# An encoder layer with a mixture of experts on one core: products that nobody reads on TensorE while it waits for the router, with four other edits around the router, the first tile and the last expert

## What is computed

```python
h = h + merged @ w_o
h = h + hier_moe(rms_norm(h, norm_ffn), w_router_group, ..., w_gate, w_up, w_down)

# hier_moe: cg, fe are the logits of 4 groups and of 8 experts in each
g_idx = jnp.argmax(cg, axis=-1)
p_e = jax.nn.softmax(fe[rows, g_idx], axis=-1)
top_p, top_i = lax.top_k(p_e, 2)
# for each of the 32 experts e, on the rows that chose it
y_e = (silu(x @ w_gate[e]) * (x @ w_up[e])) @ w_down[e]
```

## Time and profile before

| | us |
|---|---|
| median of 3 runs | 943.34 (941.81 to 944.59) |
| the profiled execution | 944.84 |
| its span, first to last instruction | 942.6 |
| PE busy | 828.6 (88%) |
| DVE busy | 269.3 (29%) |
| ACT busy | 196.9 (21%) |
| POOL busy | 133.6 (14%) |
| bytes moved by DMA | 251.41 MB, mean 267 GB/s |

### The profile page before, as it was taken

One profiled execution on the slowest core, in us unless ns is written; L12 is line 12 of the kernel. 1 busy time (PEld: TensorE's weight loads), 2 busy tenths in 40 slices (PEclk: granted clock), 3 DMA queues, 4 the chain that ended last, 5 costly groups with the idle time before them and its releaser, 6 DMA issues. The chain is left out here.

```text
span 942.6 us, 10773 instructions
## 1 busy us (share of the span) xinstructions
PE 828.6 (88%) x4578; PEld 519.3 (55%) x4578; DVE 269.3 (29%) x497; ACT 196.9 (21%) x336; POOL 133.6 (14%) x154
## 2 busy tenths in 40 slices
PE   4999998999999999997899987787877888687976
PEld 3777895679999999785434432222222333222322
DVE  4555138854313434355111110101010411001010
ACT  4423237846121313111000000000000000000000
POOL 5010061000000001210222211211111111112101
PEclk9999999989999999998699998989889989989998
DMA  9142216000203043964999999999999999999993
GB/s 321 28 141 90 90 58 226 2 2 1 105 31 134 1 179 139 404 251 154 368 413 410 410 410 410 415 406 415 413 411 410 417 415 413 409 411 416 407 416 119
DMA packets 51616, 251.41 MB, mean 267 GB/s; under 512 B 7433, under 2 KB 7481, under 8 KB 26992
## 3 DMA queue, kind: packets, MB, share of 16 engines
q1 hardware_dynamic: 39344, 228.92, 59.8%
q0 software_dynamic: 11184, 21.79, 7.9%
q10 hardware_dynamic: 1040, 0.00, 0.1%
HBM read 242.30 MB, written 15.59 MB: 274 GB/s over the span
## 5 line engine op out<-in xcount | busy, mean ns | idle before, releaser
L1377 PE MATMUL ps<-ring,xT 128*64 128x512 f32 x768 | 188.9, 648 | 50.7 <-DMA ring<-in_w_up_dram 49.7
L1377 PEld LDWEIGHTS ps<-ring,xT 128*64 128x64 f32 x768 | 60.4, 149 | 176.0 <-issue 112.0
L1767 DVE COPY hidT<-ps 128x256 f32<-128x256 f32 x32 | 13.6, 425 | 401.8 <-PE ps L1386 401.8
L1395 PE MATMUL ps<-high_ring,hidT 128*64 128x512 f32 x512 | 118.6, 604 | 7.2 <-DMA high_ring<-in_w_down_dram 2.4
L1070 PE MATMUL ps<-hnT_hi,ring_r 128*128 128x288 f32 x512 | 91.6, 296 | 0.1
L1377 PE MATMUL ps<-high_ring,xT 128*64 128x512 f32 x256 | 65.0, 667 | 18.8 <-DMA high_ring<-in_w_up_dram 18.8
L1070 PEld LDWEIGHTS ps<-hnT_hi,ring_r 128*128 128x128 f32 x512 | 75.9, 188 | 0.5 <-issue 0.5
L987 ACT ACTIVATE silu<-ps,rstd 128x256 f32<-128x256 f32 x32 | 15.2, 474 | 292.1 <-PE ps L1377 292.1
L1395 PEld LDWEIGHTS ps<-high_ring,hidT 128*64 128x64 f32 x512 | 40.6, 138 | 63.2 <-issue 60.7
L717 POOL DMA_INDIRECT out_y_dram<-yb,idx x32 | 50.3, 1572 | 147.0 <-ACT yb L991 143.2
L711 POOL DMA_INDIRECT xg<-hn_dram,idx x32 | 33.5, 1048 | 259.7 <-PE ps L1367 238.1
(11 more groups left out here) (281 smaller groups left out, 1032.3 us busy)
## 6 DMA issues: line engine op xcount, KB each, us to landing
high_ring<-in_w_down_dram SPq DMA_DIRECT2D x32, 2048.0 KB, 35.0
ring<-in_w_gate_dram SPq DMA_DIRECT2D x24, 2048.0 KB, 34.2
ring<-in_w_up_dram SPq DMA_DIRECT2D x24, 2048.0 KB, 35.2
high_ring<-in_w_gate_dram SPq DMA_DIRECT2D x8, 2048.0 KB
high_ring<-in_w_up_dram SPq DMA_DIRECT2D x8, 2048.0 KB
ring<-in_w_in_dram SPq DMA_DIRECT2D x7, 2048.0 KB, 8.7
ring<-in_w_o_dram SPq DMA_DIRECT2D x2, 2048.0 KB, 10.5
ring<-in_w_in_dram SPq DMA_DIRECT2D x2, 1024.0 KB, 8.1
```

The costliest lines, as they stand in the source:

```text
L1377: last = pe.matmul(out, xT[:, odd, k % (KD // 2), k // (KD // 2), :], w[:, k, :, s * F // 2:(s + 1) * F // 2], start=(k == 0), stop=(k == ...
L1395: last = pe.matmul(banks(6 + odd, 0, BANK, SLOTS, s * SLOTS), hidT[:, k % (KF // 2), k // (KF // 2), :], w[:, k, s * HALF_D:(s + 1) * HALF ...
```

## The change

Five edits.

1. **Products that nobody reads.** `keep_awake(n)` issues n products of two bfloat16 constants into a bank of PSUM that nothing reads: 62 in all, between the router's last steps.
2. **First tile in halves.** Tile 0 is scaled, rounded and subtracted in two halves of four chunks, ahead of the weights' pieces; chunks 0 to 3 wait for the first half only. The transposes of the next tile move inside a tile's products (after chunk 2, in tile 0 after chunk 4).
3. **First rows selected.** Expert 0's rows no longer come from the gather: `slots_first` makes a one-hot matrix `sel` per tile on VectorE, `select_tile` multiplies it with h in SBUF, ScalarE copies the rows (`xg_first`), and `wide(1)` uses them. `load_wide(4)` then stands ahead of `load_down(2)`.
4. **Last mixer tiles by halves.** The second-half products of tiles 3 and 4 are interleaved, so that chunks 0 to 3 of all tiles are done early. These chunks free the first half of pair 3's place and down 0's place (the merged arrays are now laid out in two halves), and SyncE loads both after `half_used`. The router's steps are spread anew; the product of choice and row number moves from VectorE to GpSimd (`mark_tokens`), and two instructions of `route` become one.
5. **Last expert.** `load_wide(31)` moves ahead of `load_down(29)`, and the products of gate and up of the last expert ahead of down of the expert two before it, with its own buffer `hidT_last`.

The core of the diff:

```diff
@@ SyncE
             load_wide(2)
+            sp.wait_ge(half_used, 1)
+            load_down(0)
+            wide_half(3, 0, first_half_loaded)
             sp.wait_ge(o_made, 2 * TILES)
-            load_down(0)
-            load_wide(3)
+            wide_half(3, 1, pair_loaded[3])
             load_down(1)
+            sp.wait_ge(wide_made, 1)
+            load_wide(PAIR_RING)
             sp.wait_ge(weights_made, 1)
             load_down(2)
-
-            sp.wait_ge(wide_made, 1)
-            load_wide(PAIR_RING)
...
+                    if e == EXPERTS - 2 * DOWN_RING:
+                        sp.wait_ge(wide_made, EXPERTS - PAIR_RING)
+                        load_wide(EXPERTS - 1)
@@ GpSimd
+            pool.wait_ge(eT_made, 1)
             pool.memset(xg[:, :, :], 0.0).then_inc(xg_init, 1)
...
-            gather(0)
             gather(1)
@@ ScalarE
+            act.wait_ge(rows_selected, 1)
+            act.activation(xg_first[:, :], ps[:, SELECT_BANK, :], ACT.Copy).then_inc(first_out, 1)
@@ TensorE
+            mixer_rows(3, 1, range(1))
+            turn_h(3, 0)
+            mixer_rows(3, 1, range(1, 2))
+            turn_h(2, 1)
+            mixer_rows(3, 1, range(2, 4))
+            route_tile(2, 1, 7)
+            mixer_rows(4, 1, range(0, 2))
+            route_tile(3, 0, 6)
+            rank_tile(1)
+            turn_h(4, 0)
+            mixer_rows(4, 1, range(2, 4)).then_inc(half_used, 1)
+            table_tile(0)
+            mixer_rows(3, 1, range(4, 6))
+            rank_tile(2)
+            mixer_rows(3, 1, range(6, KD))
+            route_tile(4, 0, 8)
+            mixer_rows(4, 1, range(4, 6))
+            turn_h(3, 1)
+            mixer_rows(4, 1, range(6, KD))
+            route_tile(3, 1, 9)
...
+            def select_tile(t):
+                n = TOK_ROWS[t]
+                pe.wait_ge(sel_ready, t + 1)
+                for s in range(2):
+                    last = pe.matmul(banks(SELECT_BANK, 0, BANK, SLOTS, s * SLOTS), sel[0:n, (t - 1) % TILES, :],
+                                     h[0:n, t, s * HALF_D:(s + 1) * HALF_D], start=(t == 0), stop=(t == TILES - 1),
+                                     skip_group_check=True)
...
+            def keep_awake(n):
+                for _ in range(n):
+                    pe.matmul(banks(4, 0, P), ident_b[:, :], ones[:, :], start=True, stop=True)
+
+            select_tile(0)
+            table_tile(1)
+            turn_h(4, 1)
+            select_tile(1)
+            route_tile(4, 1, 10)
+            select_tile(2)
             table_tile(2)
-            rank_tile(TILES - 1)
-            table_tile(TILES - 2)
-            table_tile(TILES - 1)
+            keep_awake(14)
+            rank_tile(3)
+            keep_awake(14)
+            select_tile(3)
+            keep_awake(14)
+            rank_tile(4)
+            select_tile(4)
+            keep_awake(8)
+            table_tile(3)
+            table_tile(4)
+            pe.wait_ge(first_out, 1)
+            for c in range(KD // 2):
+                last = pe.transpose(banks(3, c * P, (c + 1) * P), xg_first[:, c:HALF_D:KD // 2], ident[:, :])
+            last.then_inc(eT_made, 1)
+            keep_awake(12)
+            pe.wait_ge(pair_loaded[0], 32)
+            wide(1, 0, 0, xT_first[:, :, :, :])
...
+                if e == EXPERTS - 3:
+                    turn_hidden(e + 2, 1 - odd)
+                    pair_there(e + 2)
+                    wide(e + 3, odd, (e + 2) % PAIR_RING)
@@ VectorE
+            take_hn_first(0)
             split_low("k", (0,))
-            dve.wait_ge(gain_loaded, 16)
-            take_hn(0)
-            low_hn(0)
+            low_hn_first(0)
+            take_hn_first(1)
+            low_hn_first(1)
             split_low("k", (1,))
...
+            take_turned(4, 0, 8)
+            add_mixer(3, 1)
+            take_turned(3, 1, 9)
+            add_mixer(4, 1)
+            slots_first(2)
+            slots(2, 1)
+            take_turned(4, 1, 10)
+            route(3)
+            route(4)
+            for t in (3, 4):
+                slots_first(t)
+                slots(t, 1)
```

More of the change, by code:

```diff
@@ L729, in scatter @@
                 scatter_rows(idx[:, e:e + 1], e % 2, scattered[e % 2])
-            gather(0)
             gather(1)
-            for e in range(2):
-                reached(eT_made, e + 1)
-                gather(e + 2)
+            gather(2)
+            reached(eT_made, 2)
+            gather(3)
             for e in range(EXPERTS):
@@ L1303, in rank_tile @@
                 pe.wait_ge(hot_ready, t + 1)
-                if t >= 1 and t < TILES - 1:
-                    pe.wait_ge(slots_ready, min(t, TILES - 2))
-                out = banks(6, t * EXPERTS, (t + 1) * EXPERTS)
+                before = [s for s in range(t) if RANK_BANK[s] == RANK_BANK[t]]
+                if before:
+                    pe.wait_ge(slots_ready, before[-1] + 1)
+                out = banks(RANK_BANK[t], t * EXPERTS, (t + 1) * EXPERTS)
                 for s in range(t):
@@ L1324, in _ @@
                 mixer_rows(t, 0, range(KD))
-            for t in range(TILES):
+            for t in range(TILES - 2):
                 mixer_rows(t, 1, range(1))
@@ new lines, in _, with wide @@
+            turn_h(3, 1)
+            mixer_rows(4, 1, range(6, KD))
+            route_tile(3, 1, 9)
+            def wide(done, odd, pair, x=None):
+                pe.wait_ge(eT_out, done)
+                x = xT[:, odd, :, :, :] if x is None else x
+                w = pairs[pair].rearrange("p m (k n) -> p k m n", n=F)
+                for k in range(KD):
+                    for s in range(2):
+                        out = banks(2 + odd, 0, BANK, SLOTS, s * SLOTS).rearrange("p (m n) -> p m n", m=2)
+                        last = pe.matmul(out, x[:, k % (KD // 2), k // (KD // 2), :],
+                                         w[:, k, :, s * F // 2:(s + 1) * F // 2], start=(k == 0), stop=(k == KD - 1),
+                                         skip_group_check=True)
+                last.then_inc(wide_made, 1)
@@ L1368, in turn_x @@
                 last.then_inc(eT_made, 1)
-            def wide(done, odd, pair, chunks=range(KD)):
-                pe.wait_ge(eT_out, done)
-                w = pairs[pair].rearrange("p m (k n) -> p k m n", n=F)
-                for k in chunks:
-                    for s in range(2):
-                        out = banks(2 + odd, 0, BANK, SLOTS, s * SLOTS).rearrange("p (m n) -> p m n", m=2)
-                        last = pe.matmul(out, xT[:, odd, k % (KD // 2), k // (KD // 2), :],
-                                         w[:, k, :, s * F // 2:(s + 1) * F // 2], start=(k == 0), stop=(k == KD - 1),
-                                         skip_group_check=True)
-                if chunks[-1] == KD - 1:
-                    last.then_inc(wide_made, 1)
             def turn_hidden(done, odd):
```

207 lines of the change are left out of this document (143 added, 64 removed).

## The result

The changed kernel took 942.33 us (median of 20 runs, 938.15 to 946.17); the kernel before took 944.15 beside it (20 runs, 941.43 to 947.57). The ratio is 0.9976, interval 0.9964 to 0.9987. The gain is 1.8 us by the medians where 5.6 was forecast, and 942.33 lies just above the range's 942.0. (The forecast started from the 943.34 of three executions; from the 944.15 measured here the same gain would have given 938.6.) A second set of the same kernel (e11) gave 940.13 and 0.9951 (0.9931 to 0.9972). Both sets spread over 8 us and more; that spread turns out to be part of the answer.

The account below looks back on a forecast made before the run. The end was taken as the landing of the experts' last weight byte over full DMA engines, plus a tail. Weights 5.4 and tail 0.2 make 5.6 us, so 943.34 becomes 937.7, range 933.5 to 942.

Parts of the forecast that it names:

- T: End of the first expert's products, when pair 4's load is issued: forecast 457.2 us, where it was 469.1.
- The router: From the mixer's end: two route chains in sequence, selects, unread products, tables, transposes, then wide from 451.7, done at 458.8.
- the forecast's own threshold: In the slower rival (chance 0.06): first expert's products ending from 462.8 us on make the kernel slower.
- the stretch: From the mixer's end (435.2) to the issue of pair 4 (457.2): 22.0 us forecast.
- the clock falls all the same: Rival, chance 0.27: TensorE's clock drops in the wait for the second route, costing up to 5.1 us, so 942.8.
- First tile: Tile 0 in halves: first product at some 12.0 us, 1.6 us gained to the mixer's end, bounds 0 and 2.2.
- a sign of being wrong: Prediction is wrong if the first tile's lead is lost again in a stretch that VectorE or ScalarE sets.
- Mixer tiles by halves: Mixer tiles 3 and 4: half_used at 429.6, chunks done at about 436.8; the early load alone worth little.
- Unread products: Between the router's last steps on TensorE: 0.06 us each, the 14 ahead of rank 4 costing 0.8 on the path.
- Next waits: Pair 5's wait for the second expert's products: done at 469, loads lasting to 474, so hidden by 5 us.
- What the weights gain: Experts' weight loads: count as begun at 438.0 in place of 443.4, a gain of 5.4 us.
- Last expert: Kernel's tail: last down 2.3 us earlier, but scatters 5.3 to 5.9 apart; 0.2 us taken, bounds -0.5 and 2.3.

Follow-up runs that it names:

- e11: The changed kernel run again without any change, for a second profile: 940.13 us, 0.9951 of before.
- e5: Changed kernel with the old order of the last expert (wide's first half and its transposes where they stood before): 943.40 us, 0.9982 of before.
- e10: e3 with ranks and tables moved behind the logits, its pauses filled with unread products, and the last tables behind the gathered rows' transposes: 937.17 us, 0.9921 of before.
- e14: e9 run again, unchanged: 937.33 us, 0.9912 of before.
- e6: Changed kernel with 56 unread products in place of 14 behind rank 3: 939.32 us, 0.9935 of before.
- e9: e7 with more unread products around rank 4 (44 for 28 ahead, 8 behind) and 20 for 8 behind select_tile(4): 935.39 us, 0.9898 of before.
- e2: Changed kernel with down 0 and the first half of pair 3 loaded only after the mixer's last product: 942.26 us, 0.9970 of before.
- e4: Changed kernel with the first tile and the transposes among its products as before: 942.89 us, 0.9976 of before.
- e3: Changed kernel with mixer tiles 3 and 4 one after the other, route(3) beside tile 4, no early load, only 20 unread products: 941.02 us, 0.9949 of before.
- e7: Changed kernel with the router's steps in another order on TensorE and VectorE, 28 unread products ahead of rank 4: 938.56 us, 0.9931 of before.
- e12: Changed kernel's own order with all pauses filled (56 unread products behind rank 3, 8 ahead of select_tile(4), 20 behind it): 939.57 us, 0.9933 of before.
- e1: Changed kernel without its 62 unread products: 942.27 us, 0.9974 of before.
- e8: e7's order without any unread product: 940.29 us, 0.9944 of before.
- e13: Changed kernel without any unread product, a second time: 943.21 us, 0.9976 of before.

## Why the prediction was wrong

**The step that failed is T**, in "The router": "`wide` from 451.7 at full clock 7.05: T = 458.8", less 1.6. The bound it rests on (the end is T and the bytes behind it) held. From T to pair 31 it took 449.9 to 451.3 us in 13 profiles with T from 456.1 to 464.0 (all of after and the experiments but e5, where the order at the end differs, and e10); before, counted in the same way, 444.8, since there down 2 (5.1 us) had been loaded by T too. So against before T has to lie ahead of 469.13 - 5.4 = 463.7 to gain anything; the forecast's own threshold was 462.8. After has 463.98: its profile gained nothing in the weights (pair 31 there 0.3 later). Where T was as forecast, so was the time (e14 has T = 457.77 and took 937.33, forecast 457.2 and 937.7), but that match is in part luck. Beside its own before (944.81) e14 gained 7.5 us for the 5.6 forecast: 0.6 less for the later T, 1.1 more in the weights, 1.4 more in the tail (both below). The 943.34 that the forecast started from was 1.5 lower.

In after's profile T is 6.8 us late. 3.35 of that lie ahead of the stretch: the mixer ends at 438.55 where 435.2 was forecast, 2.4 of it by chance in the attention stage (e11), 0.8 because the mixer takes 68.16 for 67.3, 0.1 from the first tile. This part is not what the error hangs on: in e11 the mixer ends at 433.93, earlier than forecast, and T is still at 462.11. What is late in both profiles is the stretch, 25.4 and 28.2 for 22.0. It has two parts, both shown:

- *Work mis-sized and in the way, 2.15 us.* With the clock at 1.00 throughout the changed order takes 24.15 (e6) for 22.0. "`select_tile(3)` 0.45 (two products of `wide`'s shape, 7.04 / 32 = 0.22 each)" is the slip: `wide` issues 16 products (the section on the kernel before calls them 32, and the 8 of `down` 16, which are the records) and the trace has x32 for them, so a product of full-precision rows is two records, and a select, two products, is x4 and 1.08 us, 1.01 of it ahead of what follows. Two selects on the path are 1.1 more. `turn_h(4, 1)` stands behind `select_tile(0)` and `table_tile(1)`, 0.8 more than forecast until `route(3)` starts. The two `route` chains cost 3.2 each where 3.3 was forecast. The rest, some 0.4, is spread over rank 4, the transposes and the tables. These take 1.07 for 0.6, but they start before ScalarE's copy ends, so that unread products and tables together end 1.53 behind `select_tile(4)` where copy and tables were summed to 1.4. Another order of the same steps, with its pauses filled, takes 20.4 (e9, e14).
- *The clock, 1.3 to 4.0 us.* 25.4 in after, e2 and e4, 28.2 in e11 and e5, all with the same steps, the same 62 unread products and the same pause of 2.4 us; 24.15 where it is filled. That is the rival "the clock falls all the same", which had 0.27 of the chance and a price of up to 5.1, 2.5 for half a fall: the right mechanism, priced about right, with too small a chance. That its 942.8 lies so near to the measured 942.33 is luck, since the order's 2.15 us are not in it. The row it was judged by (a pause of 2.34 near 919 behind which `wide` took 7.09) was one draw of something that changes from one execution to the next: in e2 the `wide` behind the pause of 1.98 there took 8.78. The Trainium skill (TensorE: Matmul & The Clock Gate, "Why this matters for your kernels") warns against idle gaps between bursts of matmuls only when they are longer than the 2.42 us here. The trace does not agree with that limit, and the measurement decides: the clock fell in the stretch with 2.4 us as the longest pause (after, e2, e4, e5, e11), and with 0.77 and 0.75 as the longest (e3, e7). Of after and the experiments it stayed up in the 5 profiles with filled pauses (e6, e9, e10, e12, e14) and fell in all 10 with pauses left (after, e1 to e5, e7, e8, e11, e13). e6 kept it with pauses of 0.49 and 0.21 us left. How short a pause is safe is not shown.

Whether the unread products as the change placed them do anything stays open: the stretch without them is 27.4 and 27.6, with them 25.4 three times and 28.2 twice, and the times overlap (0.9974, 0.9976 without; 0.9976, 0.9951 with). What is shown is that enough of them to close the pause do: e12 against e13 is 3.6 us on one chip.

**The other steps.** *First tile*: first product at 12.10, as forecast 12.0; its lead was 1.47 at the pool_out weights (forecast 1.6, e4 2.0). Both compare profiles with 3.4 us of low clock behind TensorE's pause of 2.2 us near 24. That fall is chance too: of the 14 profiles with the new first tile it came in 7, which issue the pool_out weights at 134.1 to 134.5, and not in the other 7, at 132.6 to 133.0. In after's profile the lead was then lost, 2.4 us more to the next weights, which the prediction had as a sign of being wrong; but it was chance (e11, and of the other profiles only e8 has such a 117.9). *Mixer tiles by halves*: the mixer takes 68.16, 67.3 forecast, before 69.47; the early load was worth nothing, as forecast (e2). *Unread products*: 0.06 each, on the path where they stand ahead of rank 4, right. *Next waits*: pair 5 at 475.79, no hole there, right. *What the weights gain*: the formula gives pair 31 at T + 451.3, measured 450.2, so it was 1.1 us too severe. *Last expert*: 1.4 to 1.65 us and not 0.2. The scatters do set the pace, and the first goes out 12.2 us behind pair 31 as forecast (12.3); but they are 4.93 apart and not "5.3 to 5.9", and two intervals make 1.3 of the difference. It is inside the term's bounds, -0.5 to 2.3. Where the clock falls in the last `wide` (e2, e3, e8), the tail is as long as before's 28.7 all the same.

In sum for after's profile: weights +0.3, tail -1.65, together -1.4 in the span (942.6 to 941.2); forecast -5.4 and -0.2.

## What to carry to other kernels

Price a step by the row of that same operation, and count how many records one instruction leaves before dividing by them. When TensorE waits for another engine in a chain that sets the end, first put wanted work into the wait (tables, transposes, logits of the next tile) and unread products only into what is left, enough for all of it; half-filled pauses gave nothing that the times show here, filled ones 3.6 us against none at all (e12 against e13). Against the changed kernel itself, e6 and e12 have 0.9935 and 0.9933 for its 0.9976 and 0.9951. The best version found is e9/e14: the change with another order and filled pauses, 0.9898 and 0.9912 of before. Before a difference of one profile is explained, take a second profile of the same kernel.

## What the runs showed of the hardware that was not expected

- The granted clock is not fixed by the program. In the same stretch of the same kernel it was 0.50 for 3.4 us in one profile (from 454) and 10.2 us in another (from 445.6); in the stage from the pool_out weights on the same work took 117.9 and 115.0 us. Times of kernels with pauses there spread over 5 to 10 us (7 to 20 executions each), of e9 and e14 over 1.3 (6 each).
- The same pause can go either way: behind 1.94 to 1.99 us ahead of the last `wide` the clock fell in e2, e3 and e8 (`wide` 8.78) and stayed up in e1, e6, e7, e12 and e13.
- Low clock holds on under dense work: in e7 TensorE was busy 6.60 of 6.60 us at 0.50.
- With 72 unread products of 128x128 bf16 placed so that no pause over 0.2 us is left (e9, e14), the clock was 1.00 for the whole stretch; the price is 0.056 to 0.06 us each.
